# Layer norm of a hybrid decoder trunk: variance from summed squares, pair sums on VectorE, modulation shared with ScalarE

## The reference

```python
mod = silu(c) @ w_ada[l] + b_ada[l]
sh1, sc1, g1, sh2, sc2, g2 = split(mod, 6)
u = x * (1 + sc1) + sh1
x = layer_norm(ALPHA * x + (1 + g1) * mixer(u), ln_g[l, 0], ln_b[l, 0])
u = x * (1 + sc2) + sh2
f = dense_ffn(u) if l == 0 else moe_ffn(u)
x = layer_norm(ALPHA * x + (1 + g2) * f, ln_g[l, 1], ln_b[l, 1])
```

## Time and profile before

| what | value |
|---|---|
| median of 3 runs | 1350.45 us (1347.97 to 1350.59) |
| profiled execution, first to last instruction | 1347.1 us |
| TensorE matmul busy | 1296.2 us, 96% |
| VectorE, ScalarE busy | 857.1 us, 582.9 us |
| mean granted TensorE clock | 0.988 |

### The profile page before, as it was taken

One profiled execution on the slowest core, in us unless ns is written; L12 is line 12 of the kernel. 1 busy time (PEld: TensorE's weight loads), 2 busy tenths in 40 slices (PEclk: granted clock), 3 DMA queues, 4 the chain that ended last, 5 costly groups with the idle time before them and its releaser, 6 DMA issues. The chain is left out here.

```text
span 1347.1 us, 24949 instructions
## 1 busy us (share of the span) xinstructions
PE 1296.2 (96%) x10594; PEld 1091.4 (81%) x10594; DVE 857.1 (64%) x1346; ACT 582.9 (43%) x751; POOL 54.3 (4%) x104
## 2 busy tenths in 40 slices
PE   7999899999999999989999999999999999999996
PEld 3667797799999967669877999999867787876673
DVE  2678558555444457865767544644555769999896
ACT  1352334353342325334424433333335556777762
POOL 7000030000000000002100000000000000000000
PEclk8999999999999999989999999999999999999998
DMA  9666645955544553556442835634656779999990
GB/s 318 230 229 233 234 150 188 327 157 157 166 163 155 174 162 102 212 164 220 134 127 70 259 102 161 215 122 150 207 187 206 223 245 296 343 339 352 342 340 36
DMA packets 190038, 276.07 MB, mean 205 GB/s; under 512 B 7845, under 2 KB 136127, under 8 KB 184808
## 3 DMA queue, kind: packets, MB, share of 16 engines
q1 hardware_dynamic: 177856, 263.62, 58.7%
q10 hardware_dynamic: 12072, 10.86, 2.8%
HBM read 268.16 MB, written 6.30 MB: 204 GB/s over the span
## 5 line engine op out<-in xcount | busy, mean ns | idle before, releaser
L823 DVE TENSOR_TENSOR lo_raw<-raw,hi 128x2048 fp32r<-128x2048 f32 (+2 forms) x112 | 229.4, 2056 | 99.7 <-ACT hi L1933 61.0
L1933 ACT ACTIVATE hi<-raw 128x2048 fp32r<-128x2048 f32 (+2 forms) x112 | 193.6, 1728 | 113.6 <-PE bank L1095 78.2
L1063 PE MATMUL bank<-UH,hi 128*128 128x288 f32 x704 | 209.3, 297 | 0.3 <-DVE lo L2384 0.3
L1065 PE MATMUL bank<-UL,hi 128*128 128x288 f32 x704 | 207.0, 294 | 0.0
L2384 DVE TENSOR_TENSOR lo<-raw,hi 128x2048 fp32r<-128x2048 f32 (+1 forms) x42 | 95.8, 2282 | 85.6 <-ACT hi L2169 48.5
L1064 PE MATMUL bank<-UH,lo_raw 128*128 128x288 f32 x496 | 147.2, 297 | 0.0
L1063 PEld LDWEIGHTS bank<-UH,hi 128*128 128x128 f32 x704 | 132.0, 188 | 0.9 <-DVE lo L2384 0.6
L1065 PEld LDWEIGHTS bank<-UL,hi 128*128 128x128 f32 x704 | 132.5, 188 | 0.0
L1064 PE MATMUL bank<-UH,lo 128*128 128x288 f32 x432 | 127.4, 295 | 0.0
L1093 PE MATMUL bank<-hi,UGH 128*128 128x512 f32 (+9 forms) x288 | 111.7, 388 | 0.0
L1095 PE MATMUL bank<-hi,UGL 128*128 128x512 f32 (+9 forms) x288 | 107.9, 375 | 0.0
(11 more groups left out here) (497 smaller groups left out, 2690.4 us busy)
## 6 DMA issues: line engine op xcount, KB each, us to landing
raw<-in_w_ada_dram SPq DMA_DIRECT2D x48, 1024.0 KB, 7.5
raw<-in_w_in_dram SPq DMA_DIRECT2D x28, 1024.0 KB, 8.3
raw<-in_w_exp_gate_dram SPq DMA_DIRECT2D x26, 1024.0 KB, 5.9
raw<-in_w_exp_up_dram SPq DMA_DIRECT2D x26, 1024.0 KB, 7.8
raw<-in_w_exp_down_dram SPq DMA_DIRECT2D x16, 1024.0 KB, 5.2
raw<-in_w_exp_down_dram SPq DMA_DIRECT2D x16, 768.0 KB, 4.6
raw<-in_w_ff_gate_dram SPq DMA_DIRECT2D x11, 1024.0 KB, 5.5
raw<-in_w_ff_up_dram SPq DMA_DIRECT2D x11, 1024.0 KB, 5.4
```

What stands on the lines that cost most here:

```text
L823: dve.tensor_tensor(lo_x[g % XRAW][:, 0:XG[g][2] * XG[g][3]], x_raw(g), hi_x[g % XSPLIT][:, 0:XG[g][2] * XG[g][3]].bitcast(F32), ALU.subtr ...
L1063: pe.matmul(out, wh, xh, start=start, stop=False)
L1065: return pe.matmul(out, wh, xl, start=False, stop=stop)
L1933: act.activation(hi_x[q][:, 0:XG[g][2] * XG[g][3]], x_raw(g), ACT.Copy).then_inc(S("x_hi_made"), 1)
```

## The change

`lnv` is gone. The variance is now the mean of the squares less the square of the mean, so ACT squares tiles as soon as they have been added: pairs 0 to 2 during the projection's later steps (`wo` of block 1, 2 and 3) or the feed-forward's down blocks, tiles 6 and 7 one by one in `lnm`. DVE pre-adds pairs 0 to 2 of `xT` into `XSUM` and of the squares into `XSQ` (`add_up`, once for pair 1 and once for pair 2), so PE sums four tiles for each statistic, all of them in `lnm`, and none between the projection's tiles. ACT squares the mean (`MSQ`); DVE forms the variance. `UAB` is made before the mean. Quarter 3 is centred after rstd is known.

In `nu` ACT forms the wide part of u for quarters 1 to 3 (and rounds `UH` of quarter 0 straight from `xT` in the first norm); DVE keeps the wide part of quarter 0 and the small parts.

The `ada` steps move: in layer 0 the one in the first norm now follows all sums; (1, 3) runs inside `ffn`, ahead of the last down block; (1, 4) moves from after `u` into the second norm; in layer 1, (1, 10) and (1, 11) run one position earlier, ahead of `su` and of `wo` block 3, and their `adaT` comes between the two halves of block 3. Other edits: `hi_part` and `low` of the feed-forward's block 0 come one half block earlier, `hi_part` of block 1 comes before `MSQ`, the last down block's first half reports by itself (`down6_made`), the spins ahead of the feed-forward are 11 and 2 in place of 17 and 3, and `past_in` comes after Exp. `XSQ` now lies where `UL` and `UM` lie; the last down blocks use bank 2 in place of 5. The core of the diff:

```diff
-if l > 0:
-    more_ada()
...
-if l == 0:
-    more_ada()
+more_ada()
...
-s += [('wo', l, 3, 0), ('wo', l, 3, 1)]
-s.append(('lnm', l, 0))
-more_ada()
-s.append(('lnv', l, 0))
-flush()
+s.append(('wo', l, 3, 0))
+if l > 0:
+    flush()
+s += [('wo', l, 3, 1), ('lnm', l, 0)]
+if l == 0:
+    more_ada()
...
-s += [('ffn', l), ('lnm', l, 1)]
+s.append(('ffn', l))
...
-s.append(('lnv', l, 1))
...
-assert not ada
-ada += late
+s.append(('lnm', l, 1))
+more_ada()
...
+if l > 0 and q > 0:
+    pe.wait_ge(S("u_wide"), 3 * (2 * l - 1) + q)
...
-if s[2] == 3:
-    if t == 0:
-        fill(base, 6)
-    for d in (range(4), range(4, 6))[t]:
-        mean_part(d)
...
+pe.wait_ge(S("norm_dve"), norm_count(NORM_DVE, which, "sum"))
+sum_part(0, XSUM[:, 0, :], first=True)
+sum_part(0, XSUM[:, 1, :])
...
-    if d % 2 == 0:
-        pe.wait_ge(S("x_squared"), QTR * which + d // 2 + 1)
-    mm = pe.matmul(bank[7][:, 0:N], ones[:, :], XSQ[:, d, :], start=(d == 0), stop=(d == KT - 1))
-mm.then_inc(full[7], 1)
+    pe.wait_ge(read[0], base[0])
+sum_part(0, xT[:, 6, :])
+pe.wait_ge(S("x_added"), (1, 3, 4)[which])
+sum_part(0, xT[:, 7, :], last=True).then_inc(full[6], 1)
+pe.wait_ge(S("norm_dve"), norm_count(NORM_DVE, which, "sum_squares"))
+sum_part(1, XSQ[:, 0, :], first=True)
+sum_part(1, XSQ[:, 1, :])
+pe.wait_ge(S("x_squared"), 5 * which + 4)
+sum_part(1, XSQ[:, 6, :])
+pe.wait_ge(S("x_squared"), 5 * which + 5)
+sum_part(1, XSQ[:, 7, :], last=True).then_inc(full[7], 1)
...
-spin(3, 0, 17 if q == 0 else 3)
+spin(3, 0, 11 if q == 0 else 2)
...
+if (r, c, q) == (1, 1, 2):
+    for half in range(2):
+        ada_half(*IN_FFN[1:], POS[STEPS.index(IN_FFN)][0], half)
...
+if (r, c, q, t) == (1, 1, 2, 0):
+    mm.then_inc(S("down6_made"), 1)
...
-if r == 1:
-    mean_part(2 * c)
-    mean_part(2 * c + 1)
...
+if q > 0:
+    pe.wait_ge(S("u_wide"), 3 * 2 * l + q)
...
-elif k == 'u' and s[2] == 1:
+elif k == 'nu':
+    which = 2 * l + s[2]
+    U_ = U32 if s[2] == 0 else UM
+    act.wait_ge(S("norm_dve"), norm_count(NORM_DVE, which, "uab"))
+    for q in range(QTR):
+        act.wait_ge(S("norm_dve"), norm_count(NORM_DVE, which, f"scale{q}"))
+        ds = (2 * q, 2 * q + 1)
+        if q > 0:
+            for d in ds:
+                op = act.activation(U_[:, d, 0:NP_], xT[:, d, 0:NP_], ACT.Identity,
+                                    bias=UAB[:, 1, d, 0:1], scale=UAB[:, 0, d, 0:1])
+            op.then_inc(S("u_wide"), 1)
+        if which == 0:
+            if q == 0:
+                for d in ds:
+                    act.activation(UH[:, d, 0:NP_], xT[:, d, 0:NP_], ACT.Identity,
+                                   bias=UAB[:, 1, d, 0:1], scale=UAB[:, 0, d, 0:1])
+                act.wait_ge(S("u_made"), QTR * (which + 1) + q + 1)
+                act.activation(UH[:, 0:2, NP_:N], U_[:, 0:2, NP_:N], ACT.Copy).then_inc(S("uh_made"), 1)
+            else:
+                act.wait_ge(S("u_made"), QTR * (which + 1) + q + 1)
+                act.wait_ge(S("u_wide"), 3 * which + q)
+                act.activation(UH[:, 2 * q:2 * q + 2, :], U_[:, 2 * q:2 * q + 2, :],
+                               ACT.Copy).then_inc(S("uh_made"), 1)
...
+elif k == 'u' and s == ('u', 1, 1):
+    act.wait_ge(S("u_wide"), 3 * (2 * l + 1))
...
-elif k in ('pt', 'wo'):
+elif k == 'wo':
+    if s[2] > 0 and s[3] == 0:
+        if s == ('wo', 0, 3, 0):
+            act.wait_ge(full[1], base[1])
+            act.wait_ge(S("nst_stored"), 64)
+            hi_part(m + 1)
+        for b in (0, 1):
+            act.wait_ge(read[b], base[b])
+        squares(2 * s[2] - 2, 2)
+elif k == 'pt':
...
-    for b in (0, 1):
-        act.wait_ge(full[b], base[b])
-    if l == 0:
-        act.wait_ge(S("nst_stored"), 64)
-        hi_part(m)
-elif l + 1 < DEPTH:
+    act.wait_ge(read[0], base[0])
+else:
+    act.wait_ge(S("x_added"), 2)
+squares(6, 1)
+act.wait_ge(S("x_added"), (1, 3, 4)[which])
+squares(7, 1)
+if which == 0:
+    hi_part(m + 1)
+act.wait_ge(S("norm_dve"), norm_count(NORM_DVE, which, "mean"))
+act.activation(MSQ[:, :], LNM[:, :], ACT.Square).then_inc(S("norm_act"), 1)
+act.wait_ge(S("norm_dve"), norm_count(NORM_DVE, which, "var"))
+act.activation(LNR[:, :], LNR[:, :], ACT.Ln, bias=eps[:, 0:1]).then_inc(S("norm_act"), 1)
+act.wait_ge(S("norm_act"), norm_count(NORM_ACT, which, "log"))
+act.activation(LNR[:, :], LNR[:, :], ACT.Exp, scale=-0.5).then_inc(S("ln_rstd"), 1)
+if s[2] == 1:
...
-    exps()
-    for q in range(QTR):
-        act.wait_ge(S("x_centred"), QTR * (2 * l + s[2]) + q + 1)
-        act.activation(XSQ[:, 2 * q:2 * q + 2, :], xT[:, 2 * q:2 * q + 2, :], ACT.Square).then_inc(S("x_squared"), 1)
-elif k == 'lnv':
-    rsqrt(LNR[:, :], (7,), base, 1.0 / D, 0, "ln_rstd")
-    if s == ('lnv', 0, 0):
-        hi_part(m + 1)
...
+x = b - 2 * UP_CB
+if x == 0:
+    exps()
+if x in (3, 6, 9):
+    q = x // 3 - 1
+    act.wait_ge(S(f"down_read{q % 2}"), q // 2 + 2)
+    squares(2 * q, 2)
...
-def make_u(U, fac, add, q):
+def centre(q):
+    v = xT[:, 2 * q:2 * q + 2, :]
+    dve.tensor_tensor(v, v, rep(LNM[:, :], 1, 2), ALU.subtract).then_inc(S("norm_dve"), 1)
+def make_u(U, fac, add, q, wide=True):
...
-for d_ in (2 * q, 2 * q + 1):
+for d_ in (2 * q, 2 * q + 1) if wide else ():
...
+v = slice(2 * q, 2 * q + 2)
+op = dve.tensor_tensor(XSUM[:, :, :], xT[:, 0:2, :] if q == 1 else XSUM[:, :, :], xT[:, v, :], ALU.add)
+if q == 2:
+    op.then_inc(S("norm_dve"), 1)
+dve.wait_ge(S("x_squared"), 5 * which + q + 1)
+op = dve.tensor_tensor(XSQ[:, 0:2, :], XSQ[:, 0:2, :], XSQ[:, v, :], ALU.add)
+if q == 2:
+    op.then_inc(S("norm_dve"), 1)
+else:
+    then(op)
...
+if s == ('wo', 0, 3, 0):
+    low(SPLITS[m + 1][0], m + 1, 0, 0)
+if s[2] > 1 and t == 1:
+    dve.wait_ge(read[0], base[0])
+    dve.wait_ge(read[1], base[1])
+    add_up(2 * l, s[2] - 1)
...
-    got(base, 6)
-    dve.tensor_scalar(LNM[:, :], bank[6][:, 0:N], 1.0 / D, None, ALU.mult).then_inc(read[6], 1)
-    dve.wait_ge(read[6], base[6] + 1)
-    for q in range(QTR):
-        v = xT[:, 2 * q:2 * q + 2, :]
-        dve.tensor_tensor(v, v, rep(LNM[:, :], 1, 2), ALU.subtract).then_inc(S("x_centred"), 1)
-    dve.wait_ge(S("x_centred"), QTR * (2 * l + s[2] + 1))
-elif k == 'lnv':
-    if s[2] == 0:
...
+    got(base, 6)
+    dve.tensor_scalar(LNM[:, :], bank[6][:, 0:N], 1.0 / D, None, ALU.mult).then_inc(S("norm_dve"), 1)
+    dve.wait_ge(S("norm_dve"), norm_count(NORM_DVE, which, "mean"))
+    dve.nop().then_inc(read[6], 1)
+    centre(0)
+    centre(1)
+    got(base, 7)
+    dve.wait_ge(S("norm_act"), norm_count(NORM_ACT, which, "mean_squared"))
+    dve.scalar_tensor_tensor(LNR[:, :], bank[7][:, 0:N], 1.0 / D, MSQ[:, :], ALU.mult,
+                             ALU.subtract).then_inc(S("norm_dve"), 1)
+    centre(2)
+    dve.wait_ge(S("norm_dve"), norm_count(NORM_DVE, which, "var"))
+    dve.nop().then_inc(read[7], 1)
+elif k == 'nu':
+    which = 2 * l + s[2]
+    s2 = (which + 1) % 2
+    dve.wait_ge(S("norm_dve"), norm_count(NORM_DVE, which, "centre2"))
...
-    dve.tensor_tensor(v, v, rep(LNR[:, :], 1, 2), ALU.mult).then_inc(S("x_scaled_ln"), 1)
+    dve.tensor_tensor(v, v, rep(LNR[:, :], 1, 2), ALU.mult).then_inc(S("norm_dve"), 1)
+U_ = UM if s2 == 0 else U32
+def make(q):
+    dve.wait_ge(S("norm_dve"), norm_count(NORM_DVE, which, f"scale{q}"))
+    make_u(U_, UAB[:, 0, :, :], UAB[:, 1, :, :], q, wide=(q == 0))
+def lower(q):
+    if which == 0:
+        u_low(l, q)
...
-for q in range(QTR):
-    if which == 0 and q > 0:
-        scale(q)
-        u_low(l, q - 1)
-    elif which > 0 and q + 1 < QTR:
-        scale(q + 1)
-    dve.wait_ge(S("x_scaled_ln"), QTR * which + q + 1)
-    make_u(UM if s2 == 0 else U32, UAB[:, 0, :, :], UAB[:, 1, :, :], q)
-if which == 0:
-    u_low(l, QTR - 1)
+make(0)
+scale(1)
+lower(0)
+make(1)
+centre(3)
+lower(1)
+scale(2)
+make(2)
+dve.wait_ge(S("norm_dve"), norm_count(NORM_DVE, which, "centre3"))
+scale(3)
+lower(2)
+make(3)
+lower(3)
...
-dve.wait_ge(S("ffn_mm"), 2 * UP_CB + 3 * cb + 3)
+if cb > 1:
+    for x in range(2):
+        dve.wait_ge(S(f"down_read{x}"), 3 if (cb, x) == (3, 0) else 2)
+    add_up(1, cb - 1)
+if cb == 3:
+    dve.wait_ge(S("down6_made"), 1)
+else:
+    dve.wait_ge(S("ffn_mm"), 2 * UP_CB + 3 * cb + 3)
...
+if (cb, t) == (3, 1):
+    dve.wait_ge(S("ffn_mm"), 2 * UP_CB + 3 * cb + 3)
...
+if (cb, t) == (3, 0):
+    last.then_inc(S("x_added"), 1)
```

More of the change, by code:

```diff
@@ L193, in steps_of @@
     s = [('start',), ('params',)]
-    early = [(0, c) for c in range(ADA_CB)] + [(1, c) for c in range(4)]
-    late = [(1, c) for c in range(4, ADA_CB)]
-    ada = list(early)
+    ada = [(l, c) for l in range(DEPTH) for c in range(ADA_CB)]
     last = []
@@ L477, with norm_count @@
         SPLITS += [(_n + 2 * UP_CB + _b, DOWN_K[_b % 3] * 256) for _b in range(12)]
+NORM_DVE = ("sum", "sum_squares", "uab", "mean", "centre0", "centre1", "var", "centre2",
+            "scale0", "scale1", "centre3", "scale2", "scale3")
+NORM_ACT = ("mean_squared", "log")
+def norm_count(does, which, what):
```

(16 more changed lines are left out.)

67 lines of the change are left out of this document (35 added, 32 removed).

## The result

The change makes the kernel slightly slower. Its median is 1353.39 us (1347.36 to 1357.01, 20 runs) against 1350.57 us (1345.82 to 1354.24, 20 runs) for the kernel before: ratio 1.0019, 95% interval 1.001 to 1.0028. The prediction was 1341.4, range 1337.5 to 1347.5, and is off by 12 us.

What follows compares the result with a forecast made beforehand. PE, busy 96% of the span, was taken as the bound, with chains in the three norms where it works only in short pieces. Gains of 5.4, 1.8 and 1.8 make 9.0: 1350.45 less 9.0 is 1341.4, range 1337.5 to 1347.5.

Steps and rivals of the forecast that it cites:

- second norm: Norm ahead of layer 1's ba: state landed at 490.0, ba starting at 491.1; gain 1.8, bounds minus 0.3 and plus 3.8.
- upper bound of 4.8: Second norm: longest landing allowed for the state's DMAs, from the sample input's load among other loads; 2.7 was taken.
- (a): Rival: the state comes late, 4.8 or more, so the second norm gives nothing; 1343.5, chance 0.12.
- (c): Rival: TensorE's clock falls once in a new gap of PE, up to 3.4 lost; 1344.8, chance 0.14.
- first norm: Norm ahead of the feed-forward: scaling starts at 256.15, not 261.14, 5.0, plus 0.4 in the apply part; gain 5.4.
- third norm to the logits: Third norm and router: PE's bias matmul starts at 715.05, not 716.87, the rest moving along; gain 1.8, bounds 1.2 and 3.4.
- `IOTA` as the holder: Third norm: ScalarE copies IOTA only after all its wide pairs, copy ending 7.45 after the scaling, which holds PE's bias matmul.
- loads of layer 1's `w_out`: Layer 1: block 3 goes out last, at about 675.9, and is lowered by 690.1 before PE wants it; free.
- pre-adds on VectorE: First norm: two per pair-sum lie in VectorE's waits; without that cover each visit would put 1.5 on the path.
- (b): Rival: the load of the feed-forward's block 1 lands 4 later in the first norm; 1345.4, chance 0.08.
- (d): Rival: slower, the clock falls in all three norms at the full 3.4, 10.2 against 9.0; 1351.6, chance 0.04.
- (e): Rival: change isn't felt, as DVE's pre-adds or ACT's queue push the last add late by what is saved; chance 0.04.

Runs made afterwards that it cites:

- e4: The changed kernel with the ada step (1, 4) back behind u, ahead of ba, so no 1 MB loads go out beside the state's DMAs; 1349.37 us, ratio 0.9993.
- e3: The kernel before with the two DMAs of layer 1's state issued after Exp of the second norm; 1356.27 us, ratio 1.0052.
- e1: The changed kernel with layer 1's state DMAs issued right after tile 7's square in the second norm, not after Exp; 1343.45 us, ratio 0.994.
- e2: The changed kernel, state still late, with 22 filler matmuls in front of the wait in turn_past; 1347.18 us, ratio 0.9975.
- e5: e1 with ScalarE's copy of IOTA in the third norm moved ahead of its wide pairs; 1338.74 us, ratio 0.9908 to the kernel before.
- e10: e5 with ScalarE's rounding of the feed-forward's block 1 moved behind Exp of the first norm; 1337.65 us, ratio 0.9902 to the kernel before.
- e8: The kernel before with 12 filler matmuls ahead of layer 1's turn_past, meant to shift layer 1 later; 1351.53 us, ratio 1.0007.

## Why the prediction was wrong

**The step that failed** is the second norm's: "I take 2.7, nearer to the first since SP's loads only begin then: landed 490.0." It was 6.5, beyond even the upper bound of 4.8. I had seen that `past_in` moves behind Exp, that two loads of 1 MB go out in the same moment, and that PE would wait, and sized the landing by traffic in a quiet moment. e4 (3.0) and the changed kernel (6.5) show that the size of the transfer says little: its neighbours set it. By the Trainium skill ("DMA: Bandwidth & Descriptors", section "Anatomy of one DMA" and the one on latency) I had estimated 3.8 with busy memory. That too is short of 6.5, and nearer to the 4.5 of e3; the section's 2.0 is a fit for DMAs that GpSimd issues, and these two went out on ScalarE's queue.

**The second failure is that rivals (a) and (c) were taken as alternatives.** A late state is what makes PE idle, and the idle time is what lowers the clock: one chain, worth 5.1 of wait and 3.1 of half speed (e1, e2). For (c) I wrote "up to 3.4" for a fall, and that size was right for this one. A gain of 1.8 became a loss of 4.5, so 6.3 of the error is this norm. Without the late state (e1, e5) it gives 3.8, the upper bound of the prediction: from the first `w_in` load to `pb` it takes 33.6 in the kernel before, 38.1 in the changed one and 29.9 in e1 and e5. That a wait brings the clock down is also what the Trainium skill says ("TensorE: Matmul & The Clock Gate", section "HAM oscillation"), and the windows above agree, 1.00 to 0.50 within a wait of 5.7.

**The third failure is a term put at nothing**, what happens outside the three norms. The profile of the changed kernel loses 5.3 in layer 1's solver and about 1 elsewhere, and the prediction had no row for either.

Point by point:

| term | predicted gain | in the traces |
|---|---|---|
| first norm | 5.4 | 5.0 |
| second norm | 1.8 | loss of 4.5 |
| third norm to the logits | 1.8 | 0.8 |
| layer 1's solver | 0 | loss of 5.3 |
| start, layer 0, feed-forward | 0 | loss of about 1 |

These add up to the 5.0 by which the profiled execution is longer, 14.0 from the forecast span of 1338.1.

- First norm: right in size, in part by luck. `MSQ` follows the rounding of block 1 and ends at 255.23 (forecast 254.65, plus the 0.71 of late start), and ScalarE's wide pairs take 1.09 (forecast 1.04). The load took 10.0, as forecast, and was there at 252.98, just when the square of tile 7 was done. But the four square sums, forecast to end at 253.5, ended at 255.34, which less the 0.71 is 1.1 late, for the pre-adds (see below). Both branches came out together, so the error on PE's side didn't show. The part behind the scaling gained 0.2 and not 0.4 (10.4 from there to the end of the last split, 10.6 before).
- Second norm up to Exp: right. PE waits 0.72 for ScalarE's copy, and the scaling starts at 483.11, where the forecast of 487.3 less the lead of 4.0 that the kernel had there gives 483.3. (The terms there add up to 487.1; the forecast wrote 487.3. In the third norm it wrote 701.4 where the earlier trace rows have 701.31. Neither matters.)
- Third norm: `IOTA` as the holder was right, and the bias matmul did come 2.35 earlier, for the 1.8 forecast. I stopped the sum there. The clock fell behind the wait of 2.67, and the logits gained only 0.8. With `IOTA` copied early (e5) the stretch gains 4.6 (55.6 from the stores of `NSC` to the logits' copy, 60.2 before).
- Moved steps, loads of layer 1's `w_out`, pre-adds on VectorE: PE has no wait over 1 us from them. But the pre-adds didn't lie wholly in VectorE's waits, as the prediction had it: a wait of 0.91 for `XSUM` is new in the first norm, and it is what made the sums late: ScalarE's rounding of block 0, now half a block earlier, waits for its load until 245.20, and `low`, the next add and the pre-adds queue behind it.
- Rivals (b) and (d) didn't come: block 1's load took 10.0, and the clock stayed at 1.00 in the first norm.
- Rival (e), that the change isn't felt because VectorE or ScalarE push the last add late, is out: with the two new waits taken away by two small edits (e5) the kernel is 11.8 faster than before, and with e10's 12.9, more than the 9.0 forecast.

**What stays open.** The norms are explained; what the changed kernel loses ahead of them and between them isn't.

- Layer 1's solver, from the copy of `pb` to the stores of `NSC`, takes 161.3 to 161.5 in all three profiles with the old order of steps (before, e3, e8) and 162.0 to 166.6 in all ten with the new one. So it isn't only scatter between executions.
- In the changed kernel the 5.3 is made up of 3.4 more in the sum of the clock and 1.8 more of idle time of TensorE that has no releaser in the profile. In e1 and e5 the same two make 2.7 and 3.5, for 2.4 and 3.3 lost. The waits of TensorE from 500 to 665, of the kernel before and then of the changed one:

```profile
PE bank L1411 <- issue: 2.8, 1, 2.8
```

```profile
PE bank L1457 <- issue: 3.3, 2, 1.9
PE bank L1370 <- issue: 1.3, 1, 1.3
```

- The store ahead of the first norm comes at 239.2 to 241.5 in the three and at 241.2 to 246.2 in the ten, though PE's order is the same up to there. The clock's sum in layer 0's solver is 1.7 to 3.4 in the three and 3.4 to 6.8 in the ten.

Why these stops and falls are more in the new version, with the same steps in these stretches, wasn't settled; e8 was meant to tell whether phase does it, and moved the work too little. In the profiled run the solver's 5.3 is also larger than what the medians leave for it, since they lie 2.8 apart and not 5.0.

## What to carry to other kernels

When an edit issues a transfer later, look first at which large loads go out in the same moment, and size its landing by a crowded row, not by a quiet one. Where a wait on PE grows, price it twice: its length, and the half clock behind it (3.1 behind a wait of 5.7 here); fillers in front of it take the second part away, issuing the transfer early takes both. Small copies that hand a bank back belong ahead of long work in an engine's queue, as `IOTA`'s copy showed with 4.4 to 4.7 us for an edit of three lines. And compare the stretches that an edit leaves alone, too, over more than one profile: here they cost as much as a norm gives.

## What the hardware showed that was not expected

- The same 176 KB in two DMAs was usable 3.0 after its issue alone, 4.5 behind the tail of other loads and 6.5 beside two loads of 1 MB.
- After the idle stretch of the second norm the clock stayed at 0.50 until about 496, although PE had been busy without a break since 489.
- Over thirteen profiles the sum of one less the clock in layer 0's solver, with PE's order unchanged, ran from 1.7 to 6.8 us. Between two profiles this alone is as much as 5.1, more than the 2.8 between the two medians.
- In layer 1's solver TensorE stands idle in every profile with nothing to wait for that the profile shows, 2.5 us in all in e2 and 4.6 in the changed kernel and e5.
